# Output projection by token tile with the decode rows first, and one three-dimensional store per expert item

## The chip, the cores and the metric

The kernel runs on one core of a Trainium2 chip. The metric is the device time of one execution in microseconds (us); lower is better. All data is float32.

## What is computed

The reference is one inference step of a two-layer decoder trunk for 512 prompt tokens and 32 decode rows (8 sequences of 4 tokens), width 1024. Cut to what matters here, a layer is:

```python
h = x @ w_in                                    # 11 column groups of 256
y = concat([y_ret, y_swa, y_conv, y_sgu]) @ w_out   # the output projection, 1024 x 1024
x = layer_norm(DN_ALPHA * x + y, ln1_g, ln1_b)
f = hier_moe(x, ...)                            # router: 1 of 4 groups, then 2 of 8 experts in it
x = layer_norm(DN_ALPHA * x + f, ln2_g, ln2_b)
```

`hier_moe` picks two of 32 experts for each token from router logits `x @ router`; an expert is `(silu(xb @ w1) * (xb @ w3)) @ w2` with w1 and w3 of 1024 x 512 and w2 of 512 x 1024.

## The kernel before, in words

Every engine has a program of its own (`block.sync`, `block.tensor`, `block.scalar`, `block.vector`, `block.gpsimd`), and all order is written out by hand with semaphores: `E.need(name, n)` waits for a count, `E.done(ins, name)` adds to it. Each engine runs its list in order, so whatever stands behind a wait waits too. SyncE (SP) issues all weight loads, ScalarE (ACT) the stores of expert rows, GpSimd (POOL) the indirect gathers.

**Tokens** lie in five tiles: four of 128 prompt tokens and tile 4 with the 32 decode rows. **The arena** is one large buffer in which `h` (the projected columns), `x`, the ring of projection weights and the three lanes of expert weights overlap at different times.

**Projection weights** come in 1 MB chunks of 256 columns, 11 for the input projection (VAL to RG, chunks 0 to 10) and 4 for the output projection (chunks 11 to 14), through a ring: slots 0 and 1 alternate and slot 2 is used once a layer. `ring_load` waits until the chunk that held the slot is used up. `tile(c, t)` multiplies one chunk with one token tile: 8 matmuls of 256 columns for a prompt tile (L556), 32 of 64 columns for the decode tile (L561). In the profile a float32 matmul shows as two records, a transpose as one.

**Around the output projection.** The last input chunk, RG, is done tile by tile with `turn_mix` between: it transposes the gated mixer outputs of a tile into `xT` (L534, 8 transposes; ACT copies the low bank, DVE the high one). Then comes `for c in range(NCH, NCH + NOUT): for t in range(TILES)`: chunk by chunk, each chunk over all five tiles, one PSUM bank per tile. DVE adds each result to `x` (L1484) in the same order. In the last chunk it also takes the statistics of a tile (L1455, L1489, L1490), POOL raises the variance to the power -1/2 (L1780), and `row_norm` (L1461, L1464) finishes the tile before. Only after the whole projection does PE go over the five tiles once more, with `turn_rows(x_block, ..., tile_logits)`: transposes of the new `x` (L534) and eight matmuls of 40 columns a tile for the router logits (L899). DVE then routes (from L1537), while PE runs idle matmuls (L908), and SP stores `x` to `x1d` in HBM (L463).

**Expert loads ahead.** Behind the last ring load SP issues lanes 1 and 2 (six loads of 2 MB, L452), waits until the projection's last result is added, issues w1 and w3 of lane 0, the stores of `x`, and w2 of lane 0 once `x` is stored and transposed.

**The expert loop.** Tokens of an expert are cut into items of up to 32 rows; three lanes take an item each per turn. PE: `hidden` (32 matmuls, L952), `output` (16 matmuls, L970). w1, w3 and w2 of the lane's next item are loaded when `h_ps` and `y_ps` of its present one are done; if the expert is the same, the load is skipped by its condition. ACT's `rows_out` waits for `y_ps` and for the lane's previous store (`y_stored`), copies PSUM to `yo` (L1146) and stores it with four transfers (L1151), each of 32 partitions with 1 KB a row:

```python
for t in range(4):
    dst = yd[bass.ds(at, BLK), t * 256:(t + 1) * 256]
    act.dma_start(dst, yo[q][BLK * t:BLK * (t + 1), :]).then_inc(sem(f"y_stored{q}"), 16)
```

Here partition `32 t + p` of `yo` holds columns `256 t` to `256 t + 255` of item row `p`. After the loop POOL waits for all stores and gathers each token's two rows from `yd` (L1809).

Of the kernel before, what the change touches and what calls it, by code (L numbers as in the profile page):

```python
# [15 lines left out]
ALU = mybir.AluOpType  # L16
# [4 lines left out]
SEQ = 512  # L21
DEPTH = 2
NB = 8
NT = 4
NS = NB * NT
# [36 lines left out]

VAL, GATE, SQ, SK, SV, RQ, RK, V, RV, U, RG = range(NCH)
# [87 lines left out]
def offsets(fields):  # L151
    at, where = {}, 0
    for name, n in fields:
# [12 lines left out]
           smp_back=1, smp_y=1, stores=16 * 9, wout=20, wout_out=20, x1=5, x1_store=80, x1_stat=5, x1_pow=5,  # L166
# [5 lines left out]
def trunk_program(nc, io, const_at):  # L172
# [4 lines left out]
    with ctx:  # L177
# [69 lines left out]
        ring.append(arena[:, early:early + KT * CW].rearrange("p (k c) -> p k c", k=KT))  # L247
# [55 lines left out]
        def slot(c):  # L303

            return c if c < 3 else (c - 3) % 2

        def filled(c, layer):
            nth = 1 if c < 3 else (c - 3) // 2 + 2
            return (layer * (7, 7, 1)[slot(c)] + nth) * 16
# [31 lines left out]
        def _(sp):  # L341
# [12 lines left out]
            for L in range(DEPTH):  # L354
                E.L = L
                def ring_load(c):
# [69 lines left out]
                ring_load(9)  # L426
                ring_load(10)
# [14 lines left out]
                for c in range(NCH, NCH + NOUT):  # L442
                    ring_load(c)
# [23 lines left out]

# [52 lines left out]
        def _(pe):  # L520
# [3 lines left out]
            for L in range(DEPTH):  # L524
# [27 lines left out]
                def weigh(bank, c, t):  # L552
                    n = ROWS[t]
                    for k in range(KT):
                        if t < TILES - 1:
                            ins = pe.matmul(bank[0:n, 0:CW], xT[:, k, 128 * t:128 * t + n], ring[slot(c)][:, k, :],  # L556
                                            start=(k == 0), stop=(k == KT - 1))
# [1348 lines left out]
```

## Time and profile before

| | us |
|---|---|
| median of 3 runs | 1855.29 (1852.86 to 1858.3) |
| the profiled execution, its time | 1858.84 |
| its span in the profile | 1857.0 |
| PE busy | 1448.6 (78%) |
| DVE busy | 572.4 (31%) |
| ACT busy | 218.0 (12%) |
| POOL busy | 240.3 (13%) |
| data moved by DMA | 539.32 MB, mean 290 GB/s |

Layer 0 covers about 0 to 903 us and layer 1 the rest; in each the mixers and projections come first and the expert loop behind them (from 383 us and from 1281 us). A busy share is an average over stages that have different limits, so it names no bound by itself. "SPq" and "ACTq" are the engines' queues of DMA issues. A packet is one piece that one of the core's 16 DMA engines moves.

### The profile page before, as it was taken

The numbers are of one execution on the slowest core, as the hardware profiler recorded it, in microseconds if no ns is written. First come the engines' busy times: TensorE is split into PE (matmuls) and PEld (weight loads), VectorE is DVE, ScalarE is ACT, GpSimd is POOL, SyncE is SP. The second block draws the span as 40 slices with busy tenths as digits, with TensorE's granted clock in tenths as the row PEclk, the third lists the DMA queues.
The fourth block names the chain that finished last, engine by engine and source line by source line (L and its number), as shares of the span: only waits on it lengthen the run. The fifth ranks groups of instructions, "written<-read, shape, count | busy, mean of one in ns | idle before, by whom it ended". The sixth has DMA issues, their size and how long they took to land.

```text
span 1857.0 us, 40385 instructions
## 1 busy us (share of the span) xinstructions
PE 1448.6 (78%) x16476; PEld 1014.9 (55%) x16476; DVE 572.4 (31%) x1257; ACT 218.0 (12%) x615; POOL 240.3 (13%) x323
## 2 busy tenths in 40 slices
PE   8989999988577667757498999998657657756990
PEld 7767888855244334424387777886434434433550
DVE  0766652721010000001747756254000000000117
ACT  2122220100000000000112321010000000000110
POOL 2100210121011001100310003011101101101113
PEclk9999999889789788879699998989888978889995
DMA  8742134759999999999632403294999999999824
GB/s 344 272 161 104 46 108 193 309 197 403 428 425 376 427 426 426 379 424 409 212 149 105 182 25 108 78 384 181 421 426 425 381 426 424 426 425 427 325 83 146
DMA packets 79285, 539.32 MB, mean 290 GB/s; under 512 B 14671, under 2 KB 32011, under 8 KB 50411
## 3 DMA queue, kind: packets, MB, share of 16 engines
q1 hardware_dynamic: 47338, 488.68, 63.8%
q0 software_dynamic: 11136, 35.40, 5.2%
q10 hardware_dynamic: 20736, 14.18, 2.4%
q8 instruction: 55, 0.90, 0.2%
q14 instruction: 20, 0.16, 0.0%
HBM read 776.83 MB, written 38.20 MB: 439 GB/s over the span
## 4 chain that ended last, share of the span: by engine, by line
PE 50%; DMA 39%; DVE 5%; SPq 2%; issue 2%; POOL 1%; ACT 1%; ACTq 0%; DVEq 0%; POOLq 0%
DMA arena<-in_w 36%; PE ps L556 20%; PE ps L952 13%; PE ps L970 3%; PE ps L908 2%; PE ps L561 1%; DVE arena L1711 1%; PE ps L642 1%; DMA arena<-in_ret_state 1%; DVE arena L1461 1%; PE ps L534 1%; DMA arena<-in_kv 1%; PE ps L899 1%; DVE bn L1455 1%; PE ps L660 1%
## 5 line engine op out<-in xcount | busy, mean ns | idle before, releaser
L952 PE MATMUL ps<-arena,xT 128*32 128x256 f32 x6912 | 472.9, 434 | 256.0 <-DMA arena<-in_w 254.4
L952 PEld LDWEIGHTS ps<-arena,xT 128*32 128x32 f32 x6912 | 271.7, 125 | 446.6 <-issue 353.9
L556 PE MATMUL ps<-arena,xT 128*128 128x256 f32 x1920 | 450.2, 393 | 0.4 <-ACT arena L1033 0.4
L556 PEld LDWEIGHTS ps<-arena,xT 128*128 128x128 f32 x1920 | 371.2, 197 | 68.7 <-issue 15.1
L1679 DVE COPY xT<-ps 128x128 f32<-128x128 f32 x108 | 31.5, 292 | 908.6 <-PE ps L961 908.6
L970 PE MATMUL ps<-arena,xT 128*32 128x256 f32 x3456 | 212.2, 386 | 34.3 <-DVE xT L1679 22.7
L970 PEld LDWEIGHTS ps<-arena,xT 128*32 128x32 f32 x3456 | 109.1, 110 | 110.4 <-issue 29.6
L1796 POOL COPY xT<-xT 128x1 int32 x108 | 19.7, 182 | 804.1 <-PE ps L942 804.1
L1231 DVE SCALAR_TENSOR_TENSOR arena<-arena 128x784 f32<-128x784 f32 x120 | 115.3, 1028 | 0.0
L1798 POOL DMA_INDIRECT xT<-x1d,xT x108 | 105.6, 977 | 53.1 <-POOL xT L1796 50.1
L1141 ACT ACTIVATE xT<-ps 128x128 f32<-128x128 f32 x108 | 30.0, 278 | 678.8 <-PE ps L952 678.8
L1030 ACT ACTIVATE arena<-ps 128x256 f32<-128x256 f32 x88 | 33.8, 384 | 350.1 <-PE ps L556 350.1
L1146 ACT COPY xT<-ps 128x256 f32<-128x256 f32 x108 | 40.2, 373 | 280.9 <-PE ps L970 280.9
L534 PE MATMUL ps<-const,arena 128*128 128x128 f32 (+1 forms) x240 | 35.7, 300 | 39.6 <-DVE arena L1464 32.4
L1746 POOL TENSOR_TENSOR rstat<-rstat,halfc 128x5 f32<-128x5 f32 (+2 forms) x6 | 14.9, 2482 | 333.3 <-DVE rstat L1193 333.3
L1675 DVE COPY xT<-ps 128x256 f32<-128x256 f32 x114 | 48.4, 425 | 22.5 <-PE ps L942 22.5
L534 PEld LDWEIGHTS ps<-const,arena 128*128 128x128 f32 (+1 forms) x240 | 29.8, 162 | 44.6 <-DVE arena L1464 34.0
L942 PE MATMUL ps<-const,xT 128*128 128x128 f32 x228 | 44.2, 276 | 10.4 <-DMA xT<-x1d,xT 9.3
L908 PE MATMUL ps<-const 128*128 128x256 f32 x200 | 46.0, 388 | 0.0
L1020 ACT COPY xT<-ps 128x512 f32<-128x512 f32 (+1 forms) x50 | 25.0, 523 | 173.5 <-PE ps L534 172.9
L908 PEld LDWEIGHTS ps<-const 128*128 128x128 f32 x200 | 38.6, 195 | 5.6
L961 PEld LDWEIGHTS ps<-const,xT 128*128 128x128 f32 x108 | 15.0, 138 | 44.5 <-issue 44.5
(249 smaller groups left out, 1063.5 us busy)
## 6 DMA issues: line engine op xcount, KB each, us to landing
arena<-in_w SPq DMA_DIRECT2D x324, 2048.0 KB
arena<-in_w_proj SPq DMA_DIRECT2D x30, 1024.0 KB, 5.0
arena<-in_kv SPq DMA_DIRECT2D x32, 640.0 KB, 8.0
yd<-xT ACTq DMA_DIRECT2D x432, 32.0 KB, 8.1
yd<-arena POOLq DMA_DIRECT2D x22, 512.0 KB, 20.2
rowpar<-in_rowpar SPq DMA_DIRECT2D x2, 2708.0 KB, 17.2
arena<-in_x_in SPq DMA_DIRECT2D x8, 512.0 KB, 5.3
x1d<-arena SPq DMA_DIRECT2D x8, 512.0 KB, 14.5
```

Source lines behind the costliest of these rows:

```text
L534: ins = pe.transpose(ps[g][:, j * 128:j * 128 + n], source(t, 4 * g + j), ident[0:n, 0:n])
L556: ins = pe.matmul(bank[0:n, 0:CW], xT[:, k, 128 * t:128 * t + n], ring[slot(c)][:, k, :], start=(k == 0), stop=(k == KT - 1))
L908: pe.matmul(HIDDEN[:, 0:256], ident, ones2, start=True, stop=True)
L942: ins = pe.transpose(TOKENS[:, b * 128:(b + 1) * 128], xg[q][:, b * 128:(b + 1) * 128], ident)
L952: ins = pe.matmul(HB[q][r, 0:256], xgT[q][:, k % 2, BLK * (k // 2):BLK * (k // 2 + 1)], w13[q][:, :, k, 128 * j:128 * (j + 1)], start=(k = ...
L970: ins = pe.matmul(YB[q][r, 0:256], hT[q][:, BLK * c:BLK * (c + 1)], w2[q][:, c, 256 * t:256 * (t + 1)], start=(c == 0), stop=(c == 3), til ...
L1030: ins = act.activation(h[0:n, c, t, :], bank[0:n, 0:CW], func.get(c, ACT.Copy))
L1146: act.copy(yo[q], YB[q][:, 0:256]).then_inc(sem(f"y_out{q}"), 1)
L1231: ins = dve.scalar_tensor_tensor(out=acc[:, cb, :], in0=src, scalar=cw[:, cb * TAPS + j:cb * TAPS + j + 1], in1=acc[:, cb, :], op0=ALU.mul ...
L1675: dve.tensor_copy(xgT[q], TOKENS[:, 0:256].rearrange("p (b m) -> p b m", b=2)).then_inc(sem(f"xgT{q}"), 1)
L1679: dve.tensor_copy(hT[q], HIDDEN[:, 0:128]).then_inc(sem(f"hT{q}"), 1)
L1798: pool.indirect_dma_start(out=xg[q], out_offset=None, in_=x1q, in_offset=bass.IndirectOffsetOnAxis(ap=gidx[q], axis=0))\
```

## The change

Six things are edited.

1. The ring gets a fourth slot, at `HCOLS` (where the first caches of keys lay before, and lane 2 of the expert weights later). Chunk 11 goes into it, loaded before chunk 10, chunk 12 into slot 2, chunks 13 and 14 into slots 0 and 1.
2. RG, the transposes and the output projection go by token tile in the order `OUT_TILES = (4, 0, 1, 2, 3)`. A tile's four chunks are done together, two chunks to a PSUM bank, and DVE adds 512 columns at once.
3. `row_norm` of a tile follows its statistics at once. The transposes of the new `x` and the logits of earlier tiles stand between the halves of the projection; the logits go to `ps[6]`.
4. SP: lane 1 is loaded ahead as before; lane 0 and lane 2 now wait for the end of the projection's matmuls (slot 3 lies in lane 2), with the stores of `x` between.
5. An item's rows are stored by one transfer instead of four.
6. The counts of `y_stored` change from 64 to 16 per item.

```diff
+OUT_TILES = (4, 0, 1, 2, 3)
...
-        ring.append(arena[:, early:early + KT * CW].rearrange("p (k c) -> p k c", k=KT))
+        for at in (early, HCOLS):
+            ring.append(arena[:, at:at + KT * CW].rearrange("p (k c) -> p k c", k=KT))
...
-            return c if c < 3 else (c - 3) % 2
+            return c if c < 3 else (c - 3) % 2 if c < NCH else (3, 2, 0, 1)[c - NCH]
...
-                    elif 4 < c < NCH + 2:
+                    elif 4 < c < NCH:
                         E.need("proj", (c - 1) * TILES)
-                    elif c >= NCH + 2:
-                        E.need("wout", (c - 1 - NCH) * TILES)
+                    elif c == NCH:
+                        E.need("kv_used", 2 * NB)
+                    elif c == NCH + 1:
+                        E.need("ret_o", 4)
+                        E.need("smp_o", 1)
+                    elif c > NCH + 1:
+                        E.need("proj", (c - 3) * TILES)
...
                 ring_load(9)
+                ring_load(NCH)
                 ring_load(10)
...
+                ring_load(NCH + 1)
                 E.need("smp_upd", 1)
...
-                for c in range(NCH, NCH + NOUT):
+                for c in range(NCH + 2, NCH + NOUT):
                     ring_load(c)
...
-                for q in (1, 2):
-                    for j in range(3):
-                        expert_load(j, q, L * NE + q * STEP)
-                E.need("wout_out", 4 * TILES)
-                expert_load(0, 0, L * NE)
-                expert_load(1, 0, L * NE)
-                for t in range(TILES):
-                    E.need("x1", t + 1)
+                for j in range(3):
+                    expert_load(j, 1, L * NE + STEP)
+                for k, t in enumerate(OUT_TILES):
+                    if k == TILES - 1:
+                        E.need("wout", 2 * TILES)
+                        expert_load(0, 0, L * NE)
+                        expert_load(1, 0, L * NE)
+                    E.need("x1", k + 1)
                     E.done(sp.dma_start(x1d[...], x[0:ROWS[t], t, :]), "x1_store", 16)
+                expert_load(0, 2, L * NE + 2 * STEP)
                 E.need("x1_store", 16 * TILES)
                 E.need("xT_tr", 6 * TILES)
                 expert_load(2, 0, L * NE)
+                expert_load(1, 2, L * NE + 2 * STEP)
+                expert_load(2, 2, L * NE + 2 * STEP)
...
+                def out_half(place, half_):
+                    bank = ps[2 + 2 * (place % 2) + half_]
+                    if place >= 2:
+                        E.need("wout_out", 2 * (place - 2) + half_ + 1)
+                    for c in (NCH + 2 * half_, NCH + 2 * half_ + 1):
+                        if place == 0:
+                            pe.wait_ge(sem(f"ring{slot(c)}"), filled(c, L))
+                        ins = weigh(bank, c, OUT_TILES[place], ...)
+                    E.done(ins, "wout")
...
-                for c in range(NCH, NCH + NOUT):
-                    for t in range(TILES):
-                        if c == NCH:
-                            if t == 1:
-                                turn_mix(4)
-                            E.need("xT_low", TILES + t + 1)
-                            E.need("xT_high", TILES + t + 1)
-                        out_tile(c, t)
...
-                turn_rows(x_block, lambda t: E.need("x1", t + 1), tile_logits)
+                for k in range(TILES):
+                    E.need("xT_low", TILES + k + 1)
+                    E.need("xT_high", TILES + k + 1)
+                    out_half(k, 0)
+                    if k == 0:
+                        turn_mix(4)
+                    if k >= 2:
+                        tile_logits(k - 2)
+                    if k >= 1:
+                        turn_sum(k - 1)
+                    out_half(k, 1)
+                tile_logits(3)
+                turn_sum(4)
+                tile_logits(4)
...
-                    act.wait_ge(sem(f"y_stored{q}"), i * 64)
+                    act.wait_ge(sem(f"y_stored{q}"), i * 16)
...
-                    for t in range(4):
-                        dst = yd[bass.ds(at, BLK), t * 256:(t + 1) * 256]
-                        act.dma_start(dst, yo[q][BLK * t:BLK * (t + 1), :]).then_inc(sem(f"y_stored{q}"), 16)
+                    dst = yd[bass.ds(at, BLK), :].rearrange("p (t c) -> t p c", t=4)
+                    act.dma_start(dst, yo[q]).then_inc(sem(f"y_stored{q}"), 16)
...
+                for place, t in enumerate(OUT_TILES):
+                    n = ROWS[t]
+                    dve.wait_ge(sem(f"x_in{t}"), 16 * (2 * L + 2))
+                    for k in range(2):
+                        E.need("wout", 2 * place + k + 1)
...
+                        E.need("wout_out", 2 * place + k + 1)
+                        ins = half_stats(t, k)
+                    E.link(ins)
+                    E.link(dve.bn_aggr(mv[0:n, t, 0:2], bn[0:n, t, :, :]))
+                    E.done(dve.tensor_scalar(mv[0:n, t, 3:4], mv[0:n, t, 1:2], EPS, None, ALU.add), "x1_stat")
+                    row_norm(t, place, "ln1_g", "ln1_b", "x1_pow", "x1")
```

## Rows read from the trace of the kernel before

**Rows 1.** The page, the chain that ended last, by engine.

```profile
PE 50%; DMA 39%; DVE 5%; SPq 2%; issue 2%; POOL 1%; ACT 1%; ACTq 0%; DVEq 0%; POOLq 0%
```

**Rows 2.** Busy time in stretches; last three columns: granted clock, DMA share, GB/s.

```profile
408.00:866.00 458.00, 318.13 (x4582) 180.17 (x4578) 38.65 (x138) 30.28 (x93) 53.69 (x92) 0.85 0.98 409
1287.00:1732.00 445.00, 297.80 (x4360) 169.78 (x4360) 38.02 (x135) 28.61 (x88) 54.33 (x93) 0.85 1.00 419
...
1732.00:1808.00 76.00, 72.37 (x1218) 44.01 (x1221) 10.37 (x37) 7.80 (x24) 11.02 (x19) 1.00 0.46 168
```

**Rows 3.** DMA from 408 to 866 us: packets, MB, share of 16 engines; issues.

```profile
q1 hardware_dynamic: 12044, 175.31, 90.5%
q10 hardware_dynamic: 8899, 6.08, 4.2%
...
yd<-xT ACTq DMA_DIRECT2D x185, 32.0 KB, 8.5
```

**Rows 4.** DMA from 1287 to 1732 us.

```profile
q10 hardware_dynamic: 8139, 5.58, 3.9%
```

**Rows 5.** DMA from 111 to 131 us, all packets and all issues by program.

```profile
DMA packets 1822, 3.82 MB, mean 191 GB/s; under 512 B 159, under 2 KB 1309, under 8 KB 1821
...
arena<-in_kv SPq DMA_DIRECT2D x4, 640.0 KB, 6.0
out_p_k<-arena SPq DMA_DIRECT2D x1, 512.0 KB, 8.6
out_p_v<-arena SPq DMA_DIRECT2D x1, 512.0 KB, 8.8
out_s_conv<-arena SPq DMA_DIRECT2D x1, 32.0 KB, 7.9
out_s_k<-arena SPq DMA_DIRECT2D x1, 32.0 KB, 8.6
out_s_v<-arena SPq DMA_DIRECT2D x1, 32.0 KB, 7.3
out_p_conv<-arena SPq DMA_DIRECT2D x1, 30.0 KB, 7.6
```

**Rows 6.** Timeline, layer 0 around the output projection: start, duration, instructions [idle before].

```profile
272.20 1.09 PE L534 MATMUL ps<-const,arena 128*128 128x128 f32 x8
...
319.23 14.08 PE L556 MATMUL ps<-arena,xT 128*128 128x256 f32 x64
...
333.24 1.10 PE L561 MATMUL ps<-arena,xT 128*32 128x64 f32 x64
...
334.90 0.69 DVE L1455 BATCH_NORM_STATS2 bn<-arena 128x6 f32<-128x512 f32 x1
...
336.11 1.51 POOL L1780 TENSOR_TENSOR mv<-mv,halfc 128x1 f32<-128x1 f32 x1 [2.49 <-DVE mv L1490]
...
336.59 1.88 PE L899 MATMUL ps<-router_w,xT 128*128 128x40 f32 x16
...
337.26 1.28 DVE L1464 SCALAR_TENSOR_TENSOR arena<-arena,mv,rowpar 128x1024 f32<-128x1024 f32 x1
...
343.50 1.97 PE L534 MATMUL ps<-const,arena 128*128 128x128 f32 x8 [2.09 <-DVE arena L1464]
...
345.26 3.48 PE L899 MATMUL ps<-router_w,xT 128*128 128x40 f32 x16
...
349.65 4.84 PE L899 MATMUL ps<-router_w,xT 128*128 128x40 f32 x32
```

**Rows 7.** The page, DMA issues: KB each and median us to landing.

```profile
arena<-in_w_proj SPq DMA_DIRECT2D x30, 1024.0 KB, 5.0
```

**Rows 8.** Timeline, the first issues of the loop's own loads in layer 0.

```profile
389.08 50.05 SPq L452 DMA_DIRECT2D arena<-in_w  x22
```

**Rows 9.** Timeline, the end of the expert loop of layer 1.

```profile
1809.16 1.75 ACTq L1151 DMA_DIRECT2D yd<-xT  x4
1812.22 0.19 POOL L1805 TENSOR_TENSOR halfc<-halfc 128x1 f32<-128x1 f32 x1 [24.49 <-DMA yd<-xT]
```

More of the change, by code:

```diff
@@ L564, in weigh, with tile @@
                     return ins
-                def tile(c, t):
-                    if t == 0:
+                def tile(c, t, place=None):
+                    j = serial(c, t if place is None else place, True)
+                    if c < 2 and t == 0 or c > 1 and j == c * TILES:
                         pe.wait_ge(sem(f"ring{slot(c)}"), filled(c, L))
-                    j = serial(c, t, True)
                     if j >= 2:
@@ L875, in _ @@
                 E.need("conv_y", 1)
-                for t in range(2, TILES):
-                    turn_mix(t - 2)
-                    tile(RG, t)
+                for k in range(2, TILES):
+                    turn_mix(k - 2)
+                    tile(RG, OUT_TILES[k], k)
                 turn_mix(3)
-                E.need("proj_out", 55)
-                for c in range(NCH, NCH + NOUT):
-                    for t in range(TILES):
-                        if c == NCH:
-                            if t == 1:
-                                turn_mix(4)
-                            E.need("xT_low", TILES + t + 1)
-                            E.need("xT_high", TILES + t + 1)
-                        out_tile(c, t)
@@ L890, in _ @@
-                rw = router_w[:].rearrange("p (k n) -> p k n", k=KT)
-                def tile_logits(t):
-                    n = ROWS[t]
-                    E.need("xT_low", 2 * TILES + t + 1)
-                    E.need("xT_high", 2 * TILES + t + 1)
-                    if t == 0:
-                        E.need("wout_out", 16)
-                    for k in range(KT):
-                        ins = pe.matmul(ps[2][0:n, t * NLOG:(t + 1) * NLOG], xT[:, k, 128 * t:128 * t + n], rw[:, k, :],
-                                        start=(k == 0), stop=(k == KT - 1))
-                    if t == TILES - 1:
-                        E.done(ins, "logits")
@@ L904, in _, with tile_logits @@
-                turn_rows(x_block, lambda t: E.need("x1", t + 1), tile_logits)
+                rw = router_w[:].rearrange("p (k n) -> p k n", k=KT)
+                def tile_logits(place):
+                    t = OUT_TILES[place]
+                    n = ROWS[t]
+                    E.need("xT_low", 2 * TILES + place + 1)
+                    E.need("xT_high", 2 * TILES + place + 1)
+                    for k in range(KT):
+                        ins = pe.matmul(ps[6][0:n, t * NLOG:(t + 1) * NLOG], xT[:, k, 128 * t:128 * t + n], rw[:, k, :],
+                                        start=(k == 0), stop=(k == KT - 1))
+                    if place == TILES - 1:
+                        E.done(ins, "logits")
@@ L1446, in _ @@
                 gated(1)
-                for t in range(2, TILES):
-                    mix_out(t - 2)
-                    gated(t)
+                for k in range(2, TILES):
+                    mix_out(k - 2)
+                    gated(k)
                 mix_out(3)
@@ L1455, in half_stats, with row_norm @@
                     return dve.bn_stats(bn[0:n, t, k, :], x[0:n, t, k * 512:(k + 1) * 512])
-                def row_norm(t, gain, bias, pow_done, done):
+                def row_norm(t, place, gain, bias, pow_done, done):
                     n = ROWS[t]
@@ L1776, in _ @@
                 inv_root(rstat[0:NS, 36:40])
-                for t in range(TILES):
+                for k, t in enumerate(OUT_TILES):
                     n = ROWS[t]
-                    E.need("x1_stat", t + 1)
+                    E.need("x1_stat", k + 1)
                     E.done(pool.tensor_tensor(mv[0:n, t, 2:3], mv[0:n, t, 3:4], halfc[0:n, 0:1], ALU.pow), "x1_pow")
@@ L1803, in _ @@
                 for q in range(LANES):
-                    pool.wait_ge(sem(f"y_stored{q}"), (lo + more + 1) * 64)
+                    pool.wait_ge(sem(f"y_stored{q}"), (lo + more + 1) * 16)
                 E.link(pool.tensor_tensor(halfc[:, 1:2], halfc[:, 0:1], halfc[:, 2:3], ALU.mult))
```

104 lines of the change are left out of this document (44 added, 60 removed).

## The prediction

> **What bounds the kernel now.** I read the chain that ended last first: half of it is PE and 39% is DMA [rows 1], so neither engine is the bound all over and the stages have to be taken apart. The table of stretches does that [rows 2]. From 408 to 866 us and from 1287 to 1732 us the 16 DMA engines are busy 98% and 100% of the time at 409 and 419 GB/s, while PE is busy only two thirds of it: 903 us in which the expert weights are the bound, and any DMA engine that gets more work makes the kernel longer. From 1732 to 1808 us PE is busy 72 of 76 us and DMA 46%: there expert blocks repeat, loads are skipped and stores cost nothing. Outside the loops the output projection and what follows it are bound by PE and then by a chain PE, DVE, POOL, DVE, PE [rows 6].
>
> The change touches both kinds of stage: the projection, where PE's order is new, and the stores of the loop, which share the DMA engines with the weights.
>
> **Part 1, projection and logits.** Same matmuls, new order. Before, the last projection matmul ends at 333.24 + 1.10 = 334.3 us and the last logit at 349.65 + 4.84 = 354.5 us [rows 6]: a tail of 20.2 us, partly at about half pace (eight transposes take 1.97 us at 343.50 against 1.09 us at 272.20). Now four of the five transposes of x and three of the five tiles of logits move in between the halves of the projection. A float32 matmul shows as two records here, so a tile's eight logit matmuls are the row of 16, 1.88 us, and a tile-chunk of the projection is 16 records too. The moved work adds 4 x 1.09 = 4.4 us and 3 x 1.88 = 5.6 us [rows 6] to the projection: its end moves to 344.3 us. Behind it stands one tile only. DVE adds 512 columns (not in the trace; the nearest rows are 0.69 us for the statistics of the same 512 columns and 1.28 for a pass over 1024; I take 0.7), takes statistics (0.69), aggregates (about 0.5 with the gaps), POOL's power takes 1.51 beside the first pass of the norm, the second pass takes 1.28 [rows 6]: 4.8 us with the gaps. Beside that PE has one more tile of logits (1.88), then stands idle for 2.9 us. At 343.50 it had stood idle for 2.09 us and was slow, so I take that pace: transposes 1.97, a copy of 512 columns 0.6 (a little under the statistics), logits 3.48 [rows 6]: 6.0 us. The last logit comes at 344.3 + 4.8 + 6.0 = 355.1 us; decode rows transpose in less than 1.09, which takes off some 0.4: 354.7 us, as before. At full pace 1.97 + 3.48 would be 1.09 + 1.88, 2.5 us better; I take a fifth of it. So the new order fills PE's gaps but makes a longer wait at its end, for DVE and POOL, with nothing left to fill it.
>
> Could DVE be late inside? A tile's x must be ready while the next tile's first two chunks run. Four tile-chunks take 14.08 us [rows 6], so two take 7.0, against DVE's 4.8: covered. For the decode tile, which comes first, four small copies add about 1 us: still covered.
>
> The loads: chunk 11 is put before chunk 10 on SP's queue, behind a wait for the key caches, which are used up earlier than the input chunk that chunk 10 waits for, so chunk 10 and the stores of states behind it aren't held up. Chunk 12 waits for attention scratch that is free before its turn. Chunk 14 can only be issued when RG is done, and lands 5.0 us later [rows 7]. Until it is used PE has two transposes of a tile (2 x 1.09) and three decode chunks (3 x 1.10) [rows 6]: 5.5 us. So it costs nothing, with a bound of 0 to 5 us a layer if it is late.
>
> The expert loads ahead: six of the nine 2 MB loads now start at the projection's end, 344 us. With x, 12.6 MB at 419 GB/s [rows 2] takes 30 us, to about 374 us. The loop's first own load is issued at 389.08 us [rows 8], after lane 0's first item, and the last to land belong to lane 2, whose turn comes still later. Nothing waits. The stores of x land behind 4 MB, some 10 us later, and are wanted by the first gather more than 20 us after: covered by the routing. If this cover were gone, up to 12 us. The loads of the loop start with the first hidden product, so whatever the logits gain or lose comes through to the end of the layer. **Part 1: 2 x -0.5 = -1 us; bounds 2 x -2.5 = -5 and, with chunk 14 late, +8.**
>
> **Part 2, the store.** What goes: three of four issues on ACT's queue, 1.75 / 4 = 0.44 us each [rows 9]. In the loop ACT has time to spare; at the loop's end they stand before the last landing (1809.16 + 1.75 to POOL's 1812.22): -1.3 us a layer. What the one transfer does on the DMA engines is the question of this change.
>
> Today a store of 32 rows is spread over all 16 engines: four transfers of 32 rows, 128 packets of 1 KB, and 16 completions each, 64, are 192 packets an item, and 185 issues x 48 = 8880 packets agree with the 8899 counted [rows 3]. Over how many engines will the new one go? The stretch from 111 to 131 us shows that the number depends on shape [rows 5]. It holds exactly ten transfers (four key loads and six stores), and 159 packets of under 512 B, the completions. Ten times 16 would be 160. The one whose row count isn't divisible by 16 is the store of 30 rows (30 KB): it runs on 15 engines, the largest number up to 16 that divides 30. The two stores with 128 partitions outermost and a second dimension of four tiles show the full number. In the new store the HBM side is ordered `t p c`: outermost 4, then 32, then 256 columns. If the split goes by the outermost count of both sides, as these rows suggest, it runs on **four engines**, and each gets 32 rows instead of 8.
>
> The rows alone leave two readings, since none has an outermost 4: by outermost count (four engines), or by total rows, 128 (sixteen, rival A). The Trainium skill ("DMA: Bandwidth & Descriptors", section "Why a DMA increments its semaphore by 16 and not by 1") decides between them: the engine count is the largest up to 16 that divides the slowest dimension of both access patterns. By that rule the sum is the forecast's, by the other reading it is A's 1847 us; the trace agrees with the rule in its one odd shape, 15 engines for 30 rows.
>
> A weight load is complete only when its slowest engine is, so the other twelve don't help. Items in the two bound stretches: 8899 / 192 + 8139 / 192 = 46 + 42 = 88 [rows 3, 4]. 88 x 1.12 = 99 us. Idle DMA time there takes up a part: 2% of 458 us is 9 us, of which I take half, 5. The other 20 items lie where DMA isn't the bound. At the loop's end the last store takes 1.1 us longer on four engines, which returns most of the 1.3 us saved. **Part 2: +94 us; bounds 88 x 0.7 - 9 = +53 and 88 x 1.25 = +110.**
>
> **Sum**, against the profiled execution's 1858.84 us (3.6 above the median of the runs, 1855.29): -1 + 94 = +93. On the median: 1855 + 93 = **1948 us**.
>
> **The rivals.**
>
> A. *All 16 engines take the store* (the two sides are split by total rows, or reordered first). Then 48 fewer completions an item cost between 0 and 34.4 x 48 / 16 = 0.10 us less, up to 9 us over 88 items, and the loop's end gives 2 x 1.3 = 2.6. Total: 1855 - 1 - 3 - 4 = 1847 us. For it: the 128-partition side divides by 16, and the two 4-tile stores do go to 16 [rows 5]. Against it: those have 128 outermost on both sides. This is the case that ends faster. Its point: on k engines a store costs 6.1 / k us (128 x 48 ns), against 0.41 now, so it pays from 15 engines on. Chance 0.12.
>
> B. *Four engines, but the store's wait becomes a bound too.* On each of the four engines 33 packets of a store take turns with weight rows of 16 KB, which at queue 1's 90.5% x 16 x 458 / 175.31 MB = 0.038 us per KB last 0.62 us [rows 3]. A store then needs about 33 x 0.66 = 22 us where one comes every 458 / 46 = 10 us: stores pile up, ACT stands at `y_stored`, behind it the gate of the next lane and so PE and SP. While they stand, weights run out and the store finishes at once; so the work is the same, but each turn of three items may leave the four engines empty for one landing, about 1.3 us (1810.9 to 1812.2) [rows 9]. 29 turns x 1.3 = +38 us: 1986 us. Against it: other items' stores are still queued in the gap. Chance 0.15, in part inside the range.
>
> C. *Four engines, but mostly covered*, because lanes run ahead and the extra work falls where loads are skipped (blocks of one expert repeat also inside the stretches). A third of the price would be left: 1855 - 1 + 31 = 1885 us. Against it: 98% and 100% busy [rows 2]. Chance 0.07.
>
> D. *Part 1 counts after all* (-5 us with PE at full pace in its tail, or +8 with chunk 14 late), beside any of the others, chance 0.3; it moves the sum, and only beside A can it change the sign.
>
> **How the numbers follow.** The forecast has 0.66, A 0.12, B 0.15, C 0.07. The forecast's own bounds are 1855 + 53 - 5 = 1903 and 1855 + 110 + 8 = 1973; the range reaches down towards C and up to B for eight in ten: 1895 to 1990. A measurement of this kernel can tell about 0.3%, 5.6 us, from no change. A's 1847 is only 0.4% faster, so its 0.12 is split: faster 0.08, same 0.04; slower the rest, 0.88.
>
> **What would show it.** Queue 10 with about 108 x 132 = 14256 packets if four engines post completions, 108 x 144 = 15552 if sixteen do: this alone separates A from the rest. In the two stretches the DMA share drops below 0.95 and GB/s to about 409 x 0.9 = 370, though PE still waits for weights: twelve engines idle. Stores land in 20 us or more instead of 8.5. The last logit of layer 0 comes near 354 us. Stretches longer by 1.1 us an item confirm the price; a long wait of ACT's copy for a DMA of its own together with idle DMA queues would mean B. The prediction is wrong if the completions fall to 132 an item and the stretches still don't grow.

## The result, and the profile after

The changed kernel takes **1957.78 us** (median of 4 runs, 1949.79 to 1959.32), the kernel before beside it 1854.07 (4 runs): ratio 1.0539, 95% interval 1.0518 to 1.056, 104 us slower. The forecast was 1948 in a range of 1895 to 1990. The profiled execution has a span of 1957.5 us, against 1857.0 before.

The page of the kernel after: DMA queues (packets, MB, share of 16 engines), the chain that ended last by engine and by line, and the row of ACT's copy of an item's rows.

```profile
q1 hardware_dynamic: 47338, 488.68, 61.2%
q0 software_dynamic: 11136, 35.40, 5.1%
q10 hardware_dynamic: 14256, 14.16, 2.1%
...
PE 45%; DMA 25%; another core or an unknown queue 18%; DVE 4%; issue 3%; ACT 2%; POOL 1%; SPq 1%; ACTq 1%; DVEq 0%; POOLq 0%
PE ps L570 20%; DMA yd<-xT 17%; PE ps L976 8%; PE ps L994 5%; DMA arena<-in_w 4%; PE ps L575 1%; PE ps L932 1%; PE ps L548 1%; DVE arena L1730 1%; PE ps L658 1%; DMA arena<-in_ret_state 1%; DMA xT<-x1d,xT 1%; DMA arena<-in_kv 1%; ACTq L1174 1%
...
L1170 ACT COPY xT<-ps 128x256 f32<-128x256 f32 x108 | 40.2, 372 | 834.4 <-DMA yd<-xT 695.9
...
yd<-xT ACTq DMA_DIRECT2D x108, 128.0 KB
```

The first thing to read is the count of queue 10. It has 14256 packets, which is 108 items x 132: 128 rows of 1 KB and four completions. Four engines carry an item's rows. Sixteen would have made 108 x 144 = 15552. Its MB are what they were.

The second is the chain. The stores now stand in it with 17% by their own name, and with much of the 18% that the page calls an unknown queue: in the middle of the loop those pieces run up to ACT's copy, 17.71 us from 495.33 and 19.05 us from 514.27. Before, the idle time ahead of that copy was 280.9 us, ended by PE; now it stands idle for 834 us, 696 of them for an earlier store.

The stretches of the loops in which the weights were the bound, as in [rows 2]: length; PE, PEld, DVE, ACT and POOL busy; granted clock, DMA share, GB/s.

```profile
408.00:900.00 492.00, 307.62 (x4364) 171.68 (x4356) 39.05 (x131) 27.36 (x85) 51.15 (x88) 0.81 0.91 376
1330.00:1830.00 500.00, 310.05 (x4399) 171.91 (x4399) 42.15 (x136) 29.04 (x88) 56.52 (x96) 0.81 0.91 374
```

The DMA view of 408 to 900 us, by queue, with the issues of the store; as in [rows 3].

```profile
q1 hardware_dynamic: 11948, 174.07, 84.7%
q0 software_dynamic: 2112, 5.77, 3.3%
q10 hardware_dynamic: 5320, 5.28, 3.1%
...
yd<-xT ACTq DMA_DIRECT2D x42, 128.0 KB
```

A share of 91% looks as if there were room. But it is a mean over 16 engines, and queue 10 runs on four of them, so there its 3.1% is 12.4%. Those four have 84.7 + 3.3 + 12.4 = 100.4% of the stretch to do; the other twelve have 88%. (These are sums of packet times, taken as even over the engines for queues 0 and 1. Packets of two queues can overlap in the records, so a sum can pass 100%.) The packet records show the four without a division: from 408 to 900 us exactly four packets are in flight for 6.5% of the time, 32 us, against 0.2% of 408 to 866 us before; the time with none hardly changes (7.4 us, before 6.0). **The bound moved from sixteen engines to four**, and PE still waits.

ACT in the middle of the loop (timeline: start, duration, instructions, idle time before).

```profile
474.92 0.55 ACTq L1174 DMA_DIRECT2D yd<-xT  x1
...
513.06 0.37 ACT L1170 COPY xT<-ps 128x256 f32<-128x256 f32 x1 [17.58 <-DMA yd<-xT]
513.61 0.56 ACTq L1174 DMA_DIRECT2D yd<-xT  x1
...
533.35 0.37 ACT L1170 COPY xT<-ps 128x256 f32<-128x256 f32 x1 [18.86 <-DMA yd<-xT]
533.89 0.55 ACTq L1174 DMA_DIRECT2D yd<-xT  x1
```

The waits from 408 to 900 us (who waits for whom: us in all, times, longest), and PE's wait for weights before, from 408 to 866 us.

```profile
ACT xT L1170 <- DMA yd<-xT: 321.5, 21, 18.9
...
DVE xT L1702 <- ACT xT L1165: 183.6, 17, 19.0
...
PE ps L976 <- DMA arena<-in_w: 90.5, 15, 8.4
PE ps L985 <- DVE xT L1702: 80.2, 9, 12.6
```

```profile
PE ps L952 <- DMA arena<-in_w: 129.1, 25, 8.0
```

A store that took 8.5 us to land [rows 3] now takes far longer. Each lane has one store under way, so the copy at 533.35 us waits for the store issued three items earlier, at 474.92: 58 us. There a store lands every 19 to 20 us with three queued; over the whole stretch the median from issue to landing is 30 us (completions counted in the order of issues). So ACT waits for its buffer, DVE and PE for ACT, and the wait that PE showed for weights, 129 us before, is now 171 us under two names.

Outside the loops, PE at the end of the projection of layer 0 (timeline).

```profile
333.62 6.21 PE L570 MATMUL ps<-arena,xT 128*128 128x256 f32 x28
339.67 1.87 PE L905 MATMUL ps<-router_w,xT 128*128 128x40 f32 x16
344.75 1.97 PE L548 MATMUL ps<-const,arena 128*128 128x128 f32 x8 [3.22 <-DVE arena L1489]
347.49 3.61 PE L905 MATMUL ps<-router_w,xT 128*128 128x40 f32 x16 [0.77 <-ACT xT L1044]
```

Three times of every layer tell the parts apart: the last logit and the loop's first hidden product, both counted from the start of the spatial gate's last group of 32*32 products, and the loop itself, from that hidden product to the first gather of stored rows. Layer 0 / layer 1, in us, from the timelines:

| kernel | to the last logit | to the first hidden product | loop |
|---|---|---|---|
| before | 100.5 / 100.5 | 129.5 / 129.0 | 502.6 / 532.2 |
| after | 100.8 / 101.3 | 130.7 / 131.0 | 552.8 / 581.0 |
| e1, store alone | 100.5 / 98.8 | 129.4 / 128.0 | 555.9 / 575.0 |
| e2, projection alone | 99.7 / 101.2 | 129.2 / 131.0 | 499.1 / 531.7 |

The loops hold 50.2 + 48.8 = 99 of the 100.5 us between the two spans.

### The profile page after: what moved, and what is told of

Its sections match the earlier page's. It is cut to its first block, busy times and chain, and to the rows that moved or that the text cites. A ratio compares the mean times of both kernels' runs of the same rounds, so it can differ in the third digit from the quotient of the medians.

```text
span 1957.5 us, 39397 instructions
## 1 busy us (share of the span) xinstructions
PE 1451.5 (74%) x16476; PEld 1008.6 (52%) x16476; DVE 574.1 (29%) x1221; ACT 217.3 (11%) x615; POOL 243.6 (12%) x323
## 3 DMA queue, kind: packets, MB, share of 16 engines
q10 hardware_dynamic: 14256, 14.16, 2.1%
## 4 chain that ended last, share of the span: by engine, by line
PE 45%; DMA 25%; another core or an unknown queue 18%; DVE 4%; issue 3%; ACT 2%; POOL 1%; SPq 1%; ACTq 1%; DVEq 0%; POOLq 0%
PE ps L570 20%; DMA yd<-xT 17%; PE ps L976 8%; PE ps L994 5%; DMA arena<-in_w 4%; PE ps L575 1%; PE ps L932 1%; PE ps L548 1%; DVE arena L1730 1%; PE ps L658 1%; DMA arena<-in_ret_state 1%; DMA xT<-x1d,xT 1%; DMA arena<-in_kv 1%; ACTq L1174 1%
## 5 line engine op out<-in xcount | busy, mean ns | idle before, releaser
L976 PE MATMUL ps<-arena,xT 128*32 128x256 f32 x6912 | 441.5, 412 | 137.4 <-DMA arena<-in_w 136.0
L570 PE MATMUL ps<-arena,xT 128*128 128x256 f32 x1920 | 444.1, 389 | 0.4 <-ACT arena L1057 0.4
L976 PEld LDWEIGHTS ps<-arena,xT 128*32 128x32 f32 x6912 | 255.2, 120 | 313.9 <-issue 201.0
L570 PEld LDWEIGHTS ps<-arena,xT 128*128 128x128 f32 x1920 | 366.9, 194 | 65.6 <-issue 14.7
L994 PE MATMUL ps<-arena,xT 128*32 128x256 f32 x3456 | 250.7, 439 | 22.8 <-DVE xT L1698 19.9
L985 PE MATMUL ps<-const,xT 128*128 128x128 f32 x108 | 37.9, 351 | 217.9 <-DVE xT L1702 217.8
L994 PEld LDWEIGHTS ps<-arena,xT 128*32 128x32 f32 x3456 | 120.2, 124 | 123.2 <-issue 57.0
L1702 DVE TENSOR_TENSOR xT<-ps,xT 128x128 f32<-128x128 f32 x108 | 30.8, 285 | 455.1 <-ACT xT L1165 455.1
L966 PE MATMUL ps<-const,xT 128*128 128x128 f32 x228 | 50.3, 307 | 10.9 <-DMA xT<-x1d,xT 9.8
## 6 DMA issues: line engine op xcount, KB each, us to landing
yd<-xT ACTq DMA_DIRECT2D x108, 128.0 KB
```

What stands on the lines that cost most here:

```text
L570: ins = pe.matmul(bank[0:n, at * CW:(at + 1) * CW], xT[:, k, 128 * t:128 * t + n], ring[slot(c)][:, k, :], start=(k == 0), stop=(k == KT - 1))
L966: ins = pe.transpose(TOKENS[:, b * 128:(b + 1) * 128], xg[q][:, b * 128:(b + 1) * 128], ident)
L976: ins = pe.matmul(HB[q][r, 0:256], xgT[q][:, k % 2, BLK * (k // 2):BLK * (k // 2 + 1)], w13[q][:, :, k, 128 * j:128 * (j + 1)], start=(k = ...
L985: pe.transpose(HIDDEN[:, 0:128], hm[q], ident).then_inc(sem(f"hm_tr{q}"), 1)
L994: ins = pe.matmul(YB[q][r, 0:256], hT[q][:, BLK * c:BLK * (c + 1)], w2[q][:, c, 256 * t:256 * (t + 1)], start=(c == 0), stop=(c == 3), til ...
```

## The experiments

Theory 1 (the forecast): the DMA engines' work sets the time, and a store on k engines costs each of them 6.1 / k us an item. Rivals: sixteen engines and another cause; the order of turns (a store's packets each wait behind a weight row, so the store lands late and its wait is the bound); the projection's order. "Before" is the kernel before, measured again on the same chip: 1856.36 us beside e1 to e4, 1858.91 beside f1 to f4, 1857.23 beside g1 and g2.

**e1. The store alone.** The kernel before, with this one edit and its semaphore counts.

```diff
-                    for t in range(4):
-                        dst = yd[bass.ds(at, BLK), t * 256:(t + 1) * 256]
-                        act.dma_start(dst, yo[q][BLK * t:BLK * (t + 1), :]).then_inc(...)
+                    dst = yd[bass.ds(at, BLK), :].rearrange("p (t c) -> t p c", t=4)
+                    act.dma_start(dst, yo[q]).then_inc(...)
```

> The kernel before with the one-transfer store alone. Theory (a store on four engines is the whole loss): queue 10 has 14256 packets, and the time is 1957 to 1963 us, the time after plus the 2 to 5 us that the new projection order gives. Rival (late expert loads and the new order of the projection bring the loss): 1850 to 1860 us.

1957.46 us, ratio 1.057 (1.0533 to 1.0607), 14256 packets on queue 10, loops +53.3 and +42.8 us. The whole loss is the store's.

**e2. The projection alone.** The changed kernel with the four transfers of before.

> The kernel after with the four transfers put back. Theory: the projection part gains a little by itself, 1848 to 1853 us, 2 to 6 us under the kernel before; the last logit of layer 0 stays at about 351 us. Rival (the projection part is what costs): 1900 us and more.

1857.62 us, ratio 1.001 (0.9993 to 1.0028). The expected gain of 2 to 6 us was missed: the new order is worth nothing that shows. That isn't because nothing happened in it: see the points below.

**e3. One transfer, sixteen engines.** The changed kernel, with the row outermost on both sides. An item's rows then lie in another order in the scratch block, so layer 1 works on other values.

```diff
-                    dst = yd[bass.ds(at, BLK), :].rearrange("p (t c) -> t p c", t=4)
+                    dst = yd[bass.ds(at, BLK), :].rearrange("p (t c) -> (p t) c", t=4)
```

> The kernel after with the same single transfer of 128 pieces of 1 KB, but into one contiguous block of the item, outermost count 128. The rows of an item then lie in another order in memory; bytes and pieces are the same. Theory (the outermost count sets the number of engines): 16 engines, queue 10 has 108 x 144 = 15552 packets, 1845 to 1850 us, a little under the run with four transfers, since 48 completions an item are gone. Rival (one large transfer an item is what costs, wherever it runs): 1950 us and more.

The DMA view of the page of e3:

```profile
q10 hardware_dynamic: 15552, 14.16, 2.2%
...
yd<-xT ACTq DMA_DIRECT2D x108, 128.0 KB, 9.4
```

1846.22 us, ratio 0.9947 (0.993 to 0.9965). 15552 packets are 108 x 144, sixteen completions an item. The same bytes from the same buffer in one transfer: with 128 outermost the loss is gone. The loop of layer 0 takes 499.4 us against e2's 499.1, so one issue and 48 fewer completions gain nothing there. The kernel's gain comes in the loop of layer 1 alone (519.9 against 531.7), where the layer works on other values. It isn't the store's: f1 below has one store on sixteen engines too, with the values of the kernel after, and its loop of layer 1 takes 531.0. That other values meet the experts in another order is the likely reason; it wasn't looked into. So that e3's time fell into the expected 1845 to 1850 us is chance. The places in memory are no rival either: the four transfers of before write the same rows of 1 KB to the same places as the kernel after.

**e4. Two transfers, two engines.** The changed kernel with the item in two transfers, each with two tiles outermost.

```diff
+                    for u in range(2):
+                        dst = yd[bass.ds(at, BLK), u*512:(u+1)*512].rearrange("p (t c) -> t p c", t=2)
+                        act.dma_start(dst, yo[q][2*BLK*u:2*BLK*(u+1), :]).then_inc(...)
```

> The kernel after with two transfers an item, each of 64 partitions with an outermost count of 2. Theory: both run on the same two engines; an item costs each of them 64 x 48 ns = 3.1 us against 0.41 us with sixteen, 2.7 us more on 88 items or more: 2060 to 2110 us; queue 10 has 108 x 132 = 14256 packets. Rival (the number of transfers matters, not the engines): between the kernel before and the kernel after.

2060.58 us, ratio 1.1107 (1.1068 to 1.1146). The page of e4, queue 10 and the chain; then ACT from 500 to 560 us (timeline).

```profile
q10 hardware_dynamic: 14256, 14.16, 2.0%
...
PE 47%; ACTq 34%; DMA 8%; DVE 4%; issue 3%; ACT 2%; POOL 1%; SPq 1%; DVEq 0%; POOLq 0%
```

```profile
516.00 0.37 ACT L1170 COPY xT<-ps 128x256 f32<-128x256 f32 x1 [2.29 <-PE ps L994]
516.55 17.92 ACTq L1175 DMA_DIRECT2D yd<-xT  x2
```

The packet count is that of four engines, because two transfers post two completions each. The packet records tell that it is half as many engines: from 408 to 950 us exactly two packets are in flight for 15.0% of the time (81 us) and never fewer. By theory 1 an item costs 6.10 / 2 = 3.05 us on each of the two against 0.41, so +2.64 x 46 = +121 us in the loop of layer 0; it grew by 101.4. The direction and most of the size hold, the factor is 0.83 of it. Here the wait has moved into the issue itself: two issues take 17.92 us, with ACT standing in them. Why the price of a packet, worked out from busy time, is too high here isn't settled; the sum for the two engines from 408 to 950 us is 77.4 + 3.1 + 8 x 3.0 = 104.5%, so overlapping packet times may be a part of it.

**f1 and f2. Work, or turns?** ACT copies the four tiles side by side into 32 partitions, 4 KB each, and the store has 32 packets of 4 KB instead of 128 of 1 KB: in f1 on sixteen engines, in f2 on four. Bytes an engine are as in e3 and in the changed kernel, turns a quarter. In f2 the rows of an item lie in another order.

```diff
-            yo.append(flat[:, a + 896:a + 1152])
+            yo.append(arena[BLK * q:BLK * (q + 1), ARENA - D:ARENA])
...
-                    act.copy(yo[q], YB[q][:, 0:256]).then_inc(sem(f"y_out{q}"), 1)
+                    for t in range(4):
+                        ins = act.copy(yo[q][:, t*256:(t+1)*256], YB[q][BLK*t:BLK*(t+1), 0:256])
+                    ins.then_inc(sem(f"y_out{q}"), 1)
...
f1+                  act.dma_start(yd[bass.ds(at, BLK), :], yo[q])
f2+                  dst = yd[bass.ds(at, BLK), :].rearrange("(b a) n -> a b n", a=4)
f2+                  act.dma_start(dst, yo[q])
```

> The kernel after, but ScalarE copies an item's result with four copies into 32 partitions of 1024 columns, and one transfer stores 32 pieces of 4 KB (outermost count 32: 16 engines). Theory: queue 10 has 108 x 48 = 5184 packets, an item costs each engine 2 x 0.16 us instead of 12 packets and 0.41 us; with the projection part at nothing 1843 to 1849 us, clearly under the kernel before. Rival (the longer way through ScalarE, some 1.1 us an item, holds PE up where loads are skipped): 1856 us and more.

> As f1_wide16, but the 32 pieces of 4 KB go out with an outermost count of 4, so on four engines; rows of an item lie in another order in memory. Same bytes on four engines as in the kernel after, 9 packets on each instead of 33. Theory 1 (the bytes on the four engines are the price): about 1.35 us an item on each of them, 0.95 more than before, 1925 to 1945 us. Theory 2 (the turns with weight rows of 16 KB are the price, each packet waiting for one row): 9 turns take 5.6 us where an item comes every 10 us, so nothing piles up and the time is below 1880 us.

Queue 10 on the page of f1, with the landing of its stores:

```profile
q10 hardware_dynamic: 5184, 14.16, 2.1%
...
yd<-arena ACTq DMA_DIRECT2D x108, 128.0 KB, 6.1
```

The DMA view of f2 from 408 to 866 us, and PE's wait for weights there:

```profile
q1 hardware_dynamic: 11267, 164.04, 85.3%
q0 software_dynamic: 2064, 5.64, 3.5%
q10 hardware_dynamic: 1578, 5.76, 3.1%
```

```profile
PE ps L976 <- DMA arena<-in_w: 150.9, 26, 8.9
ACT arena L1171 <- PE ps L994: 103.9, 43, 2.6
```

f1: 1858.49 us, ratio 1.0003 (0.9994 to 1.0012), a miss for both theories, which wanted 1843 to 1849. f2: 1942.38 us, ratio 1.046 (1.0445 to 1.0475), its loop of layer 0 37 us over f1's. **f2 decides**: with nine packets an engine instead of 33, ACT's copy waits for PE only (2.6 us at most), no store is late for anyone (they land 9.8 us after their issue in the median, 12.0 at most), and the loss is there all the same. Exactly four packets are in flight for 7.9% of the stretch, 36 us. The four engines have 85.3 + 3.5 + 4 x 3.1 = 101.2% to do. Had the turns been the price, f2 would have stood near f1. Its item costs 1.8% x 16 x 1939 us / 108 = 5.17 us of engine time, 1.29 on each of four: +0.88 x 46 = +40 us, measured 37.

What f1 lacks is in its queue line. Its share fell only from 2.4% (before) to 2.1%: 5.8 us of engine time an item against 6.6, which is 0.05 us an item on sixteen engines, 4 us over the 88 bound items. Beside e2's 1.001 a gain of 4 us, 0.2%, can't be told from none. With 8.5 ns a completion (below), the 32 rows cost (5.79 - 16 x 0.0085) / 32 = 177 ns each, 44 ns a KB, where the 1 KB rows cost 47.

**f3 and f4. The projection's tail.** f3 is e2 with the decode rows last. The decode tile's products pass through a scratch that lies in lane 0's weight area, so with decode rows last lane 0's loads have to wait for that scratch too; that is the second line of the edit. f4 is e2 with seven idle matmuls in PE's last wait.

```diff
f3 -OUT_TILES = (4, 0, 1, 2, 3)
f3 +OUT_TILES = (0, 1, 2, 3, 4)
f3 -                        E.need("wout", 2 * TILES)
f3 +                        E.need("wout_out", 2 * TILES)
f4                  tile_logits(3)
f4 +                for k in range(7):
f4 +                    pe.matmul(ps[7][:, 0:256], ident, const[:, const_at["ones"][0]:const_at["ones"][0] + 256], start=True, stop=True)
f4                  turn_sum(4)
```

> The kernel after with four transfers (e2_proj_only) and OUT_TILES = (0, 1, 2, 3, 4); lane 0's first load then waits for the last result to be added, since the decode rows' scratch lies there. Theory: the decode tile's four small copies (1.18 us for each half) come into the tail, its transposes and logits are shorter (0.68 and 0.76 us at full pace against 1.09 and 1.88): the last logit comes within 1.5 us of e2_proj_only and the time within 0.3% of it, 1850 to 1862 us. Rival (decode rows first is what keeps the tail short): 5 us and more over e2_proj_only.

> The kernel after with four transfers (e2_proj_only) and seven idle matmuls of 256 columns (0.44 to 0.49 us each) in PE's last wait of the projection, 3.22 us at 341.5 us of layer 0. Theory (the tail is slow because PE stood idle): transposes 1.09 and logits 1.88 us instead of 1.97 and 3.6, the last logit 2 to 3 us earlier in each layer, 1848 to 1853 us. Rival (the pace of the tail does not hang on that wait): no change beyond 0.1%.

PE's tail in layer 0, e2 first, then f3, then f4 (timelines).

```profile
344.69 1.97 PE L548 MATMUL ps<-const,arena 128*128 128x128 f32 x8 [3.21 <-DVE arena L1490]
347.43 3.61 PE L905 MATMUL ps<-router_w,xT 128*128 128x40 f32 x16 [0.77 <-ACT xT L1044]
```

```profile
349.14 1.06 PE L548 MATMUL ps<-const,arena 32*128 32x32 f32 x8 [4.20 <-DVE arena L1490]
350.65 1.24 PE L905 MATMUL ps<-router_w,xT 128*32 128x40 f32 x16 [0.45 <-ACT xT L1044]
```

```profile
344.88 3.27 PE L928 MATMUL ps<-const 128*128 128x256 f32 x14
348.27 1.09 PE L548 MATMUL ps<-const,arena 128*128 128x128 f32 x8
350.19 1.95 PE L905 MATMUL ps<-router_w,xT 128*128 128x40 f32 x16 [0.82 <-ACT xT L1046]
```

f3: 1854.14 us, ratio 0.9977 (0.9968 to 0.9986). f4: 1855.87 us, ratio 0.9987 (0.9975 to 0.9999). In f4 the same transposes and logits take 3.04 us instead of 5.58, at a granted clock of 1.00 (2.4 GHz) where e2 has 0.50 (1.2 GHz): the slow pace of the tail came from the idle time ahead of it, as the forecast had taken it. In f3 they take 2.30 at the slow pace (0.50), because the tile behind the wait has 32 rows. Against the kernel before f3 gains 0.2% and f4 0.1% (its interval ends at 0.9999); f4's expected 1848 to 1853 us was missed.

**g1 and g2. Both together, and f3 again.** g1 is f3 with eight idle matmuls, g2 is f3.

> Order tile by tile with the decode rows last, four transfers as before, and eight idle matmuls of 256 columns in PE's last wait of the projection. If what each of the two gave by itself adds up (decode rows last 0.9977, idle matmuls 0.9987 against 1.001 with neither), the ratio to the kernel before is 0.9977 - 0.0023 = 0.9954, about 1850 us. If they overlap, because the last tile behind the wait is now 32 rows and its transposes and logits cost 2.3 us in all at either pace, the idle matmuls save at most 1 us a layer and the ratio stays at 0.9977 to 0.9966. In the trace transposes and logits of the last tile take less than 1.06 and 1.24 us if the pace is the point.

> The same without the idle matmuls, once more on this chip: 0.9977 again if the decode rows' place is worth 0.2%; 1.000 if that was chance.

The tail of g1 in layer 0 (timeline):

```profile
347.22 3.70 PE L928 MATMUL ps<-const 128*128 128x256 f32 x16
351.60 0.68 PE L548 MATMUL ps<-const,arena 32*128 32x32 f32 x8 [0.68 <-DVE arena L1492]
352.73 0.73 PE L905 MATMUL ps<-router_w,xT 128*32 128x40 f32 x16 [0.45 <-ACT xT L1046]
```

g1: 1850.99 us, ratio 0.997 (0.9959 to 0.9982). g2: 1853.67 us, ratio 0.998 (0.9969 to 0.9991), f3's again. The gains overlap: the idle matmuls shorten the transposes and logits of the tail in layer 0 from 2.30 to 1.41 us (granted clock 1.00 against 0.50). The two kernels' intervals overlap, so the idle matmuls aren't shown to gain anything here. In the traces the last logit comes 0.8 us earlier than in g2 in layer 1 and 1.8 us later in layer 0, where g1's profiled execution, the longest of its nine, ran from 253 to 263 us at a granted clock of 0.72 (g2: 1.00) behind a wait of 2.30 us for DVE. The best version of the study is the new projection with decode rows last, four transfers, and the idle matmuls: 0.3% faster than the kernel before, which is as little as can be told from no change here. The projection's order is worth keeping only in this form, and the store not at all.

## Why the prediction was right, point by point

**How many engines.** Right: 14256 packets, the number given for four engines; rival A's 15552 appeared only in e3, where 128 is outermost on both sides. The Trainium skill ("DMA: Bandwidth & Descriptors", section "Why a DMA increments its semaphore by 16 and not by 1") takes the largest number up to 16 that divides the slowest dimension of both patterns; the counts of the kernel after (4), of e3 (16), of f1 (32 outermost, 48 packets an item: 16 engines) and f2 (36 packets: 4) agree with it, and this is what decided between the forecast and A.

**The price of a packet.** Right. Two kernels with the same rows and other completions give both unknowns. Before: 2.4% x 16 x 1857 us / 108 = 6.60 us of engine time an item for 128 rows and 64 completions; after: 2.1% x 16 x 1957.5 / 108 = 6.09 for 128 and 4. The difference, 0.51 us over 60 completions, is 8.5 ns each, and a row costs 47.3 ns. (The shares are rounded to 0.1%, so the completion may be 4 to 13 ns; the row moves by less than 2.) The single packet records say the same: 9.0 ns in the mean for a completion, 47.2 for a row of the kernel after and 47.8 for one before. The forecast took 48 between 34.4 and 51.6, near the end at which completions are free. An item on four engines: 6.09 / 4 = 1.52 us, so +1.11 us; forecast +1.12.

**88 items on the bound path.** Right in layer 0, where 46 x 1.11 = 51 us and the loop grew by 50.2; in layer 1, 42 x 1.11 = 47 and it grew by 48.8. Rival C (mostly covered) would have shown a third of that.

**Part 1.** Right as a sum, in part by luck. Predicted and measured in layer 0, relative to the same point of the layer: the projection's end 10 us later, measured 9.2 (from 80.4 to 89.6); the tail from there to the last logit 10.8, measured 11.3; DVE and POOL between them 4.8, measured 4.8 (339.87 to 344.70); transposes and logits 1.97 and 3.48, measured 1.97 and 3.61. The last logit came 0.3 us later than before, predicted 0.2 (at 351.1 us by the clock of the trace and not at 354.7, because the whole layer stands 3.7 us earlier in this execution). The recorded -0.5 us a layer takes off the hoped-for faster pace and leaves out this 0.2; by its own terms it should be -0.3. e2 prices all of it at 1.001, so the gain of rival D didn't come. (The loads ahead are 14.8 MB with `x`, and 12.6 without, so 35 us and not 30; PE's first hidden product waited for DVE and not for them.)

The luck is in the 9.2. The moved work was priced at 10.0, with full tiles and whole durations; from start to start it takes 7.4 (transposes 0.61 + 3 x 0.91, logits 0.69 + 2 x 1.71, one tile of each being the decode rows). Some 0.9 more is a slow stretch at the start: from 247.7 to 252.8 us the granted clock was 0.67, behind a wait of 2.30 us for DVE. The rest is a gap of 0.94 us that nobody had priced. It isn't chunk 14, which landed at 273.84 us and was first used at 274.29, at most 0.2 us behind the last matmul of chunk 13: it stands inside the chunk, before the last 7 of its 32 matmuls, where the program waits for nothing.

```profile
276.20 0.42 PE L575 MATMUL ps<-arena,xT 128*32 128x64 f32 x14 [0.94 <-issue]
```

In layer 1 this gap is 2.71 us, so the projection ends 9.8 us later than before. The traces of the kernel after, e2, e3, f1, f2 and f4 have 13 such gaps over 0.5 us, and in each PE goes on 1.2 to 1.5 us after a packet of 16 KB on queue 8, which the page calls "instruction", has landed. That reads as PE waiting for its own code; no run tries it. The traces with decode rows last (f3, g1, g2) have none, so a part of f3's gain may be this.

f4 shows both things. With PE kept busy the last logit of layer 0 came 2.4 us earlier than in e2 (97.3 against 99.7). In layer 1 it came no earlier (101.6 against 101.2), though the tail was as fast there (1.09 and 1.95 us): a second gap had opened in the projection, which ended 2.6 us later than e2's.

```profile
1180.39 5.45 PE L570 MATMUL ps<-arena,xT 128*128 128x256 f32 x24 [2.27 <-issue]
```

**Rival B, the wait at `y_stored`.** Its place was right and its price wrong. The wait appeared as it described (17.6 to 18.9 us in the timeline above, ACT first, then DVE and PE), a store comes out every 19 to 20 us in the middle of the loop where its arithmetic said 22, and the chain of waits reads as if it were the cause. But its sign was idle DMA queues beside that wait, and there are none: the four engines are at 100.4%, and from 495.3 to 533.3 us, over two such waits, at least 16 packets are in flight for 93% of the time and never fewer than four. f2 takes the wait away and keeps the loss. The +38 us that B put on top isn't there.

**Where the 10 us are that the forecast lacked** (+93 forecast, +104 measured on the medians, +100.5 between spans). The term "idle DMA time takes up 5 us" was mis-sized: the loops gave nothing back, 99 us against 94. The time without a packet in flight is as long as before (7.4 and 6.0 us in the stretch of layer 0). The loop's end was priced as even (1.1 us longer, 1.3 saved). In layer 1 the last store now lands 2.9 us after its issue instead of 1.3, and the end from issue to POOL costs 0.4 us more than before; in layer 0 it is even (3.66 us against 3.72).

The rest, about 1 us a layer, lies between the last logit and the first hidden product (28.9 and 28.4 us before, 29.9 and 29.7 after), and the forecast had nothing there. The traces show where. Behind the last logit stands a fixed run of idle matmuls, 36 records, and PE goes from it to the next product of the routing without a wait, so it is the run that is late. Layer 0, before and after (timelines):

```profile
354.42 8.86 PE L908 MATMUL ps<-const 128*128 128x256 f32 x36
```

```profile
350.90 9.93 PE L932 MATMUL ps<-const 128*128 128x256 f32 x36
```

Over them the granted clock was 0.90 before and 0.80 after; in layer 1 they took 8.84 and 10.15 us. The clock fell to 0.50 in PE's wait ahead of the last tile, and its records have it there until 356.1 us before and until 354.8 after: 1.7 us of the run lie in it before and 3.9 after. The run is longer by 1.1 and 1.3 us, the way to the first hidden product by 0.9 and 1.3. In f4's layer 0, at 1.00, they took 8.02 us and PE waited for DVE behind them. So the price of the longer wait goes on behind the logits.

The end of the loop of layer 1 (timelines of ACT and POOL), against [rows 9]:

```profile
1909.43 0.55 ACTq L1174 DMA_DIRECT2D yd<-xT  x1
```

```profile
1912.91 0.19 POOL L1824 TENSOR_TENSOR halfc<-halfc 128x1 f32<-128x1 f32 x1 [24.83 <-DMA yd<-xT]
```

## What to carry to other kernels

Before transfers are merged, look at what stands outermost on both sides: it sets how many DMA engines carry the bytes, and the packet count of the queue, taken for one transfer, tells which it was. Beside a stream that fills all engines, a small transfer on four of them costs the whole stream its work divided by four: 2.1% of the DMA time on average was 5% of the kernel. A DMA share of 0.91 can hide four full engines, so multiply each queue's share by 16 over its number of engines; and when the longest wait in the chain is a new one, take it away (as f2 did) before calling it the cause.

## What was not expected

**Packets of 4 KB gave nothing that shows.** f1's cost 44 ns a KB against 47 for 1 KB rows, and the kernel stayed at 1.0003, though its further copies on ACT (1.49 us an item in place of 0.37) lie in time that ACT has to spare, and DMA share and GB/s from 408 to 866 us are those of before, 0.98 and 409. The Trainium skill ("Perfetto Trace Analysis", section "DMA Optimizations") says that transfers under 2 KB carry a large overhead and that batching them into 4 KB or more can raise throughput a lot. It speaks of the size of whole transfers; if it is read of packets, these stores, 128 KB in one transfer, don't show it: 7% less time a byte in packets four times as large.

**The layer after is part of the measurement.** e3 would have passed for a gain of 0.5% by the store. Its layer 0, where the data are the same, shows no such gain.

**Idle time has a price behind it, but not each time.** After 3.2 us of standing still PE ran eight transposes in 1.97 us, and in 1.09 when it had been kept busy. Yet filling the wait moved the whole kernel by 0.1 to 0.2% only, since one tile stood behind it. And the gap of 2.70 us inside e2's projection of layer 1 cost its own length alone: behind it, from 1171.2 to 1180 us, the granted clock stayed at 1.00. Why the one wait lowers the clock and the other doesn't wasn't tried.
